# Two transformer blocks on one core: row norms taken by halves of the columns, and the first column tile of the index queries loaded in two contraction halves

## The chip, the core and the metric

The kernel runs on one core of one Trainium2 chip. The metric is the device time of one execution in microseconds (us), taken as the median of several runs. Less is better.

## The reference

Two layers on 256 rows `x` of 1,024 columns, all in float32. Cut to what matters here:

```python
h = rmsnorm(x, g_pre)
... = split_cols(h @ w_in)            # 11,352 columns: index queries iq (512), and 14 more
merged = s_gla * (y_gla @ w_gla_out) + s_dsa * (y_dsa @ w_dsa_out) + s_mem * (y_mem @ w_x_out)
x = x + rmsnorm(merged @ w_o, g_post) # end of the first block
h = rms_norm(x, mix_norm_gain_2)      # start of the second block
...
x = x + merged_2 @ w_out
h2 = rms_norm(x, ffn_norm_gain_2)
x = x + (silu(gate) * up) @ w_down
out = rms_norm(x, final_norm_gain_2)
```

`rmsnorm(x, g)` is `x * rsqrt(mean(x * x over the 1,024 columns) + 1e-6) * g`, row by row. The change touches the norm at the start, the two at the end of the first block (`wo` and `y`), the one ahead of the feed-forward part (`f`), the last one (`o`), and the first projection of the index queries.

## The kernel before, in words

The 256 rows are two row tiles (t = 0, 1) of 128 partitions by 1,024 columns: `xres` holds the residual, `xn` the normalised rows. All weights, about 130 MB, come from memory once. A weight unit (1 MB, 2,048 columns on 128 partitions; some are smaller) is loaded by SyncE (line 1226) into one of five ring slots (`NSLOT`); SyncE issues the load of unit i when TensorE has used unit i - 5. Every unit is then split in two parts for a product that keeps float32 precision: ScalarE writes the high part `w_hi` (`highs`, line 1331, three buffers), VectorE the low part `w_lo` (`lows`, line 1811), and TensorE multiplies three times (`three`, lines 505 to 507: high by high, high by low, low by high). The order of work on each engine is written out by hand: `bank_ready(name)` on ScalarE and VectorE first splits the units up to two past the one that fills the bank `name`, then waits for the bank. `full(name)` is the semaphore of a filled PSUM bank, `read(name)` that of a bank read out.

**A norm** goes through four engines. ScalarE squares a row tile with an accumulator (`squares`, line 1316, plus the read of the accumulator), GpSimd makes `rstd` in two instructions on 128x1 (`rsqrt_mean`: line 1714, multiply and add, then line 1715, power), VectorE multiplies the rows (`scale_rows`, line 1840), and TensorE transposes them, eight 128x128 pieces per row tile (`transpose_tokens`, line 570). ScalarE then writes the high part of the transposed rows with the gain (`high_of_transposed`, line 1354) and VectorE the low part (`low_of_transposed`, line 1848); the products follow.

- **Start.** VectorE copies the transposed parameters first (bank `par0`, line 1862), then scales both row tiles. Unit `small` (0.5 MB, 128 columns) is multiplied first, then `iq0` (1 MB), then small transposes (`ik2`), the transposes of the normalised memory rows (tag `m`), and `iq1`. `project_channels` has the two 128-column tiles c as outer loop and the eight contraction tiles inside.
- **Middle.** `wo0` and `wo1` fill four banks, column half c by row tile t. ScalarE copies them into `xn` (line 1346) and squares a whole row tile when both halves are copied. VectorE multiplies by `rstd` and `g_post` (line 2095) and adds to `xres` (line 2096), which gives `x_mid`. Then the norm `y` on `xres`: `squares`, `rsqrt_mean`, `scale_rows`, transposes, and the products `beta` and `c0` to `c5`, whose results feed a convolution on VectorE. SyncE waits for `x_mid` before it stores the rows and before it loads the units behind `c2` (line 1267).
- **Norm f.** VectorE adds the banks `w2o{c}{t}` into `xres` (line 2402), then the norm.
- **Close.** VectorE adds the banks `wd{c}{t}` into `xres` (line 2431), ScalarE squares each row tile (line 1316), GpSimd makes `rstd`, VectorE writes the result in one instruction for each row tile (line 2435), and SyncE stores it, 512 KB at a time (line 1277).

## Time and profile before

| | |
|---|---|
| median of 3 runs | 929.31 us (929.09 to 931.03) |
| the profiled execution's own time | 927.24 us |
| its span, first to last instruction | 925.4 us |
| TensorE busy | 883.6 us, 95% of the span |
| VectorE busy | 549.7 us, 59% |
| ScalarE busy | 426.5 us, 46% |
| GpSimd busy | 49.7 us, 5% |
| chain that ended last, by engine | TensorE 87%, VectorE 8%, ScalarE 2%, issue 1%, GpSimd 1% |
| granted TensorE clock, mean | 0.988 of full |

TensorE works for all but 41.8 us of the span. The profile also says, for each engine, what it waited for, and shows the instructions in order of time; PE is TensorE's matmuls, DVE is VectorE, ACT is ScalarE, POOL is GpSimd, SPq the queue of SyncE. A line number is one of the kernel before.

### The profile page before, as it was taken

Reading aid. Unit: us, or ns where it says so; the run is one execution under the profiler, and the core shown is the slowest. Engines: PE = TensorE matmul, PEld = TensorE weight load, DVE = VectorE, ACT = ScalarE, POOL = GpSimd, SP = SyncE. Lnnn points to the kernel's source line nnn. Section 1 sums busy time; section 2 is a strip of 40 time slices with the busy share of each in tenths; the row PEclk is TensorE's granted clock in tenths of the full one; section 3 lists DMA queues with packets and bytes.
Section 4 is the critical chain, followed back from the end, with each engine's and each line's share of the span. In section 5 each row is a group of like instructions: output and inputs, shape, how many; then the busy total and the mean of one; then the engine's idle time right before and its main releaser. Section 6 shows DMA issues by size and latency. Waiting matters only on the chain.

```text
span 925.4 us, 13903 instructions
## 1 busy us (share of the span) xinstructions
PE 883.6 (95%) x5834; PEld 773.4 (84%) x5834; DVE 549.7 (59%) x798; ACT 426.5 (46%) x577; POOL 49.7 (5%) x72
## 2 busy tenths in 40 slices
PE   5999999999999999999789999899989899999996
PEld 5998999899998888888679998677877688888885
DVE  4755564573647665654469878754366556666442
ACT  6644444744345444444446515754434444444341
POOL 1000000000020110000010151000000000000000
PEclk9999999999999999999989999999999999999998
DMA  9557743455454544555557665004554465555441
GB/s 302 171 195 221 230 143 137 137 182 182 138 160 160 181 164 155 182 204 198 166 185 161 160 137 184 1 3 139 148 213 149 158 192 190 188 188 185 159 159 46
DMA packets 127492, 151.67 MB, mean 164 GB/s; under 512 B 16919, under 2 KB 93078, under 8 KB 127430
## 3 DMA queue, kind: packets, MB, share of 16 engines
q1 hardware_dynamic: 127290, 150.70, 51.1%
q8 instruction: 46, 0.75, 0.3%
q14 instruction: 16, 0.13, 0.1%
q0 software_dynamic: 64, 0.07, 0.0%
q10 hardware_dynamic: 76, 0.02, 0.0%
HBM read 148.67 MB, written 3.68 MB: 165 GB/s over the span
## 4 chain that ended last, share of the span: by engine, by line
PE 87%; DVE 8%; ACT 2%; issue 1%; POOL 1%; DMA 0%; ACTq 0%; POOLq 0%; DVEq 0%
PE bank L505 25%; PE bank L507 24%; PE bank L506 24%; DVE w_lo L1811 2%; DVE arena L2151 1%; PE bank L570 1%; PE bank L750 1%; ACT w_hi L1331 1%; PE bank L651 1%; PE bank L631 1%; PE bank L975 1%; PE bank L880 1%; PE bank L994 1%; PE bank L1170 1%; ACT h_hi L1354 1%
## 5 line engine op out<-in xcount | busy, mean ns | idle before, releaser
L1811 DVE TENSOR_TENSOR w_lo<-ring,w_hi 128x2048 fp32r<-128x2048 f32 (+2 forms) x133 | 300.7, 2265 | 194.7 <-ACT w_hi L1331 194.5
L1331 ACT ACTIVATE w_hi<-ring 128x2048 fp32r<-128x2048 f32 (+2 forms) x133 | 250.0, 1881 | 138.4 <-PE bank L507 125.8
L505 PE MATMUL bank<-h_hi,w_hi 128*128 128x256 f32 (+1 forms) x640 | 184.9, 289 | 4.0 <-DVE w_lo L1811 2.4
L506 PE MATMUL bank<-h_lo,w_hi 128*128 128x256 f32 (+1 forms) x640 | 181.7, 284 | 0.0
L507 PE MATMUL bank<-h_hi,w_lo 128*128 128x256 f32 (+1 forms) x640 | 181.6, 284 | 0.0
L505 PE MATMUL bank<-w_hi,h_hi 128*128 128x512 f32 (+1 forms) x400 | 155.7, 389 | 0.7 <-DVE h_lo L1848 0.7
L507 PE MATMUL bank<-w_hi,h_lo 128*128 128x512 f32 (+1 forms) x400 | 152.6, 381 | 0.0
L506 PE MATMUL bank<-w_lo,h_hi 128*128 128x512 f32 (+1 forms) x400 | 152.4, 381 | 0.0
L505 PEld LDWEIGHTS bank<-h_hi,w_hi 128*128 128x128 f32 (+1 forms) x640 | 122.8, 192 | 6.8 <-issue 3.3
L506 PEld LDWEIGHTS bank<-h_lo,w_hi 128*128 128x128 f32 (+1 forms) x640 | 123.0, 192 | 0.6 <-issue 0.5
L507 PEld LDWEIGHTS bank<-h_hi,w_lo 128*128 128x128 f32 (+1 forms) x640 | 123.0, 192 | 0.0
L1346 ACT ACTIVATE arena<-bank 128x512 f32<-128x512 f32 (+5 forms) x95 | 48.5, 526 | 110.1 <-PE bank L507 95.4
L505 PEld LDWEIGHTS bank<-w_hi,h_hi 128*128 128x128 f32 x400 | 75.2, 188 | 15.7 <-issue 1.8
L507 PEld LDWEIGHTS bank<-w_hi,h_lo 128*128 128x128 f32 x400 | 75.2, 188 | 14.7
L506 PEld LDWEIGHTS bank<-w_lo,h_hi 128*128 128x128 f32 x400 | 75.3, 188 | 13.7
L1378 ACT ACTIVATE arena<-bank 128x512 f32<-128x512 f32 (+1 forms) x48 | 23.8, 499 | 96.7 <-PE bank L507 96.7
L1714 POOL TENSOR_SCALAR arena<-arena 128x1 f32<-128x1 f32 (+2 forms) x17 | 5.6, 330 | 666.1 <-ACT arena L1316 373.2
L505 PE MATMUL bank<-w_hi,y_hi 128*128 128x512 f32 x96 | 38.6, 402 | 1.2 <-DVE w_lo L1811 1.2
L507 PE MATMUL bank<-w_hi,y_lo 128*128 128x512 f32 x96 | 37.5, 391 | 0.0
L506 PE MATMUL bank<-w_lo,y_hi 128*128 128x512 f32 x96 | 37.5, 390 | 0.0
L1499 ACT ACTIVATE arena<-arena 128x128 f32<-128x128 f32 (+1 forms) x48 | 21.3, 444 | 32.7 <-DVE arena L2027 32.7
L505 PE MATMUL bank<-w_hi,f_hi 128*128 128x512 f32 x88 | 34.3, 390 | 0.0
(311 smaller groups left out, 1198.9 us busy)
## 6 DMA issues: line engine op xcount, KB each, us to landing
ring<-in_w_in SPq DMA_DIRECT2D x60, 1024.0 KB, 4.9
ring<-in_w_gate_up SPq DMA_DIRECT2D x44, 512.0 KB, 4.6
ring<-in_w_down SPq DMA_DIRECT2D x10, 1024.0 KB, 4.9
ring<-in_w_mem_kv SPq DMA_DIRECT2D x8, 1024.0 KB, 6.2
ring<-in_w_gla_out SPq DMA_DIRECT2D x4, 1024.0 KB, 4.9
ring<-in_w_x_out SPq DMA_DIRECT2D x4, 1024.0 KB, 4.9
ring<-in_w_dsa_out SPq DMA_DIRECT2D x4, 1024.0 KB, 5.4
ring<-in_w_o SPq DMA_DIRECT2D x4, 1024.0 KB, 4.9
```

The source lines that it names most:

```text
L505: mm(o, ah, bh, start=start, stop=False, skip_group_check=True)
L506: mm(o, ah, bl, start=False, stop=False, skip_group_check=True)
L507: return mm(o, al, bh, start=False, stop=stop, skip_group_check=True)
L570: ins = nc.tensor.transpose(bank_of(f"T{tag}{j}")[:, 256 * kk + 128 * t:256 * kk + 128 * t + 128], src[:, t, 128 * k:128 * k + 128], ident)
L631: ins = mm(bank[:, 256 * t:256 * t + 256], xq[:, 2 * h + c, 128 * t:128 * t + 128], mk[:, 2 * h + c, :], start=c == 0, stop=c == 1)
L651: ins = mm(bank[:, 256 * c:256 * c + 256], mv[:, m, at:at + 128], probT[:, h % 3, 256 * m:256 * m + 256], start=m == 0, stop=m == 1)
L750: ins = nc.tensor.transpose(bank[:, a:a + 128], rows[:, a:a + 128], ident)
L1331: act(w_hi[:, k % NHI, 0:m], ring[:, order.index(name) % NSLOT, 0:m], ACT.Copy)\
L1346: act(dst, src, ACT.Copy, scale=1.0 if scale is None else scale).then_inc(inc or bank_reader(name), 1)
L1378: act(tnh[:, i % 2, 0:n], src, ACT.Tanh, scale=0.5).then_inc(inc or signal("tanh_done"), 1)
L1499: ins = act(v, v, ACT.Exp, bias=neg_max[:, c:c + 1], scale=-1.0, accum_out=p_sum[:, c:c + 1])
L1811: tt_(w_lo[:, i, 0:m], ring[:, i, 0:m], w_hi[:, k % NHI, 0:m].bitcast(F), ALU.subtract)\
```

## The change

Three edits, one in each of the matters below, and the order of the work around them.

- **Norms by halves.** For `wo`, `y` of the second row tile, `f` and `o`, ScalarE squares 512 columns at a time (`half_squares`). For `wo` it reads the PSUM banks themselves, and the copies into `xn` are gone. GpSimd takes the first half's sum with the 1e-6 (`rsqrt_first`) and adds the second half's to it ahead of the power (`rsqrt_second`): one more 128x1 instruction for each norm and row tile.
- **Gain ahead of the factor.** In the middle VectorE multiplies the bank by `g_post` (`wo_gain`), and then does `xn * rstd + xres` in one instruction for each half (`x_in_the_middle`). At the close it multiplies by the last gain as each bank comes, and the last step is `result`, a multiplication by `rstd` for each half; SyncE stores 256 KB at a time, four times. In `f` and `o` the first halves' sums of both row tiles stand ahead of the second halves'.
- **Start.** VectorE scales row tile 0 ahead of the copy of `par0`. The unit `iq0` becomes `iq0a` and `iq0b`, contraction tiles 0 to 3 and 4 to 7, 0.5 MB each and each in its own ring slot, and `project_channels_by_parts` has the contraction tile as outer loop and the column tile inside. The matmuls are the same in number and shape. All later units sit one ring slot further on.

```diff
-        units_of("iq", w1, W1_OFF["iq"], 2)
+        for half in range(2):
+            unit(f"iq0{'ab'[half]}", piece(w1, W1_OFF["iq"], 256, 0, 4 * half, 4 * half + 4))
+        units_of("iq", w1, W1_OFF["iq"] + 256, 1, 1)
...
+            def project_channels_by_parts(name, x):
+
+                bank = open_bank(name)
+                for part, k0 in (("a", 0), ("b", 4)):
+                    wh, wl = split_unit(name + part, 256)
+                    for k in range(k0, k0 + 4):
+                        for c in range(2):
+                            s = slice(128 * c, 128 * c + 128)
+                            ins = three(bank[:, 256 * c:256 * c + 256], (wh[:, k - k0, s], wl[:, k - k0, s]),
+                                        (x[0][:, k, :], x[1][:, k, :]), k == 0 and c == 0, k == KT - 1)
+                    if part == "a":
+                        part_done(name + part, ins)
+                done(name, ins)
+                unit_used[name + "b"] = full(name)
...
-            project_channels("iq0", h_parts)
+            project_channels_by_parts("iq0", h_parts)
...
-                    sp.wait_ge(signal("x_mid"), 2)
+                    sp.wait_ge(signal("x_mid"), 4)
...
-                sp.wait_ge(signal("result"), t + 1)
-                sp.dma_start(out[0, 128 * t:128 * t + 128, :], xn[:, t, :]).then_inc(signal("out_done"), 16)
-            sp.wait_ge(signal("out_done"), 32)
+                for c in range(2):
+                    sp.wait_ge(signal("result"), 2 * t + c + 1)
+                    sp.dma_start(out[0, 128 * t:128 * t + 128, 512 * c:512 * c + 512], xn[:, t, 512 * c:512 * c + 512])\
+                        .then_inc(signal("out_done"), 16)
+            sp.wait_ge(signal("out_done"), 64)
...
+            def half_squares(tag, src, col, c, t):
+
+                n = square_count[tag] = square_count.get(tag, 0) + 1
+                i = col + 2 * c + t
+                act(probT[:, c, :], src, ACT.Square, accum_out=sumsq[:, i:i + 1]).then_inc(signal(f"sumsq_{tag}"), 1)
+                sc.wait_ge(signal(f"sumsq_{tag}"), n)
...
+            sc.wait_ge(*read("par0"))
             high_of_transposed("x", h_hi)
-            highs(2)
+            highs(3)
...
-            copy_wide("wo0", xn, 0)
-            for t in range(TT):
-                copy(f"wo1{t}", xn[:, t, 512:1024])
-                squares("wo", xn, 4, t, read(f"wo1{t}"))
-            highs(splits_by["wo11"] + 2)
-            for t in range(TT):
-                squares("y", xres, 0, t, (signal("x_mid"), t + 1))
+            for c in range(2):
+                for t in range(TT):
+                    bank_ready(f"wo{c}{t}")
+                    half_squares("wo", bank_of(f"wo{c}{t}")[:, :], 4, c, t)
+            squares("y", xres, 2, 0, (signal("x_mid"), 2))
+            square_count["y"] = 1
+            for c in range(2):
+                sc.wait_ge(signal("x_mid"), c + 3)
+                half_squares("y", xres[:, 1, 512 * c:512 * c + 512], 0, c, 1)
...
-            highs(splits_by["w2o11"] + 2)
-            for t in range(TT):
-                squares("f", xres, 4, t, read(f"w2o1{t}"))
+            for c in range(2):
+                for t in range(TT):
+                    highs(splits_by[f"w2o{c}{t}"] + 2)
+                    sc.wait_ge(*read(f"w2o{c}{t}"))
+                    half_squares("f", xres[:, t, 512 * c:512 * c + 512], 4, c, t)
...
-                squares("o", xres, 6, t, read(f"wd1{t}"))
+            for c in range(2):
+                for t in range(TT):
+                    sc.wait_ge(*read(f"wd{c}{t}"))
+                    half_squares("o", xres[:, t, 512 * c:512 * c + 512], 0, c, t)
...
+            def rsqrt_first(tag, col, t, n):
+
+                gp.wait_ge(signal(f"sumsq_{tag}"), n)
+                step(nc.gpsimd.tensor_scalar(var[:, col + t:col + t + 1], sumsq[:, col + t:col + t + 1], 1 / D, EPS,
+                                             ALU.mult, ALU.add))
+
+            def rsqrt_second(tag, col, t, n):
+
+                i = slice(col + 2 + t, col + 3 + t)
+                gp.wait_ge(signal(f"sumsq_{tag}"), n)
+                step(nc.gpsimd.tensor_scalar(var[:, i], sumsq[:, i], 1 / D, var[:, col + t:col + t + 1], ALU.mult, ALU.add))
+                nc.gpsimd.tensor_tensor(rstd[:, i], var[:, i], mhalf, ALU.pow).then_inc(signal(f"rstd_{tag}"), 1)
...
-            for t in range(TT):
-                rsqrt_mean("wo", 4 + t, 1, D, t + 1)
-            for t in range(TT):
-                rsqrt_mean("y", t, 1, D, t + 1)
+            rsqrt_first("wo", 4, 0, 1)
+            rsqrt_first("wo", 4, 1, 2)
+            rsqrt_second("wo", 4, 0, 3)
+            rsqrt_second("wo", 4, 1, 4)
+            rsqrt_mean("y", 2, 1, D, 1)
+            rsqrt_first("y", 0, 1, 2)
+            rsqrt_second("y", 0, 1, 3)
...
+            for name, col in (("f", 4), ("o", 0)):
+                for t in range(TT):
+                    rsqrt_first(name, col, t, t + 1)
+                for t in range(TT):
+                    rsqrt_second(name, col, t, TT + t + 1)
...
+            scale_tile("x", xn, xres, 0, 0)
             ve.wait_ge(*full("par0"))
             nc.vector.tensor_copy(par[:, 0:38], bank_of("par0")[:, 0:38]).then_inc(reader("par0"), 1)
+            scale_tile("x", xn, xres, 0, 1)
             ve.wait_ge(*read("par0"))
             tsc(g_gla_half, g_gla, 0.5, None, ALU.mult)
-            scale_rows("x", xn, xres, 0)
             lows(1)
             low_of_transposed("x", h_lo, h_hi)
-            lows(2)
+            lows(3)
...
+            def wo_gain(c, t):
+                s = slice(512 * c, 512 * c + 512)
+                ve.wait_ge(signal("sumsq_wo"), 2 * c + t + 1)
+                tt_(xn[:, t, s], bank_of(f"wo{c}{t}")[:, :], g_post[:, s], ALU.mult).then_inc(reader(f"wo{c}{t}"), 1)
+
+            def x_in_the_middle(t):
+                r = rstd_of("wo", 6, t)
+                for c in range(2):
+                    s = slice(512 * c, 512 * c + 512)
+                    ve.wait_ge(*read(f"wo{c}{t}"))
+                    stt(xres[:, t, s], xn[:, t, s], r, xres[:, t, s], ALU.mult, ALU.add).then_inc(signal("x_mid"), 1)
+
+            ve.wait_ge(signal("g_post_in"), 16)
+            for t in range(TT):
+                bank_ready(f"wo0{t}")
+                wo_gain(0, t)
+            lows(splits_by["wo11"] + 1)
+            ve.wait_ge(signal("x_again"), 16)
+            wo_gain(1, 0)
+            x_in_the_middle(0)
+            wo_gain(1, 1)
+            x_in_the_middle(1)
+            ve.wait_ge(signal("x_mid"), 4)
+            scale_tile("y", xn, xres, 2, 0)
+            scale_tile("y", xn, xres, 2, 1)
             lows(splits_by["wo11"] + 2)
-            ve.wait_ge(signal("g_post_in"), 16)
-            ve.wait_ge(signal("x_again"), 16)
-            for t in range(TT):
-                r = rstd_of("wo", 4, t)
-                step(stt(xn[:, t, :], xn[:, t, :], r, g_post, ALU.mult, ALU.mult))
-                tt_(xres[:, t, :], xres[:, t, :], xn[:, t, :], ALU.add).then_inc(signal("x_mid"), 1)
-
-
-            scale_rows("y", xn, xres, 0)
...
-            lows(splits_by["Tf3"] + 2)
-            scale_rows("f", xn, xres, 4)
+            scale_rows("f", xn, xres, 6)
...
+            ve.wait_ge(signal("g_fin_in"), 16)
+
+            def result(t):
+                r = rstd_of("o", 2, t)
+                for c in range(2):
+                    o = xn[:, t, 512 * c:512 * c + 512]
+                    tsc(o, o, r, None, ALU.mult).then_inc(signal("result"), 1)
+
             for c in range(2):
+                s = slice(512 * c, 512 * c + 512)
                 for t in range(TT):
                     bank_ready(f"wd{c}{t}")
-                    v = xres[:, t, 512 * c:512 * c + 512]
+                    v = xres[:, t, s]
                     tt_(v, v, bank_of(f"wd{c}{t}")[:, :], ALU.add).then_inc(reader(f"wd{c}{t}"), 1)
-            ve.wait_ge(signal("g_fin_in"), 16)
+                    ve.wait_ge(*read(f"wd{c}{t}"))
+                    step(tt_(xn[:, t, s], v, g_fin[:, s], ALU.mult))
             for t in range(TT):
-                r = rstd_of("o", 6, t)
-                stt(xn[:, t, :], xres[:, t, :], r, g_fin, ALU.mult, ALU.mult).then_inc(signal("result"), 1)
+                result(t)
```

VectorE's instructions at the start, from the parameters' copy to the memory rows (x4 and the like count equal rows; `w_lo<-ring,w_hi` is a unit's low part, `h_lo` the low part of the transposed rows). Before:

```order
L1862 COPY arena<-bank 128x38
L1864 TENSOR_SCALAR arena<-arena 128x2
L1840 TENSOR_SCALAR arena<-arena 128x1024 x2
L1811 TENSOR_TENSOR w_lo<-ring,w_hi 128x1024
L1848 SCALAR_TENSOR_TENSOR h_lo<-bank,arena,h_hi 128x256 x8
L1811 TENSOR_TENSOR w_lo<-ring,w_hi 128x2048
L1840 TENSOR_SCALAR arena<-arena 128x1024 x2
```

The same place in the changed kernel:

```order
L1891 TENSOR_SCALAR arena<-arena 128x1024
L1918 COPY arena<-bank 128x38
L1891 TENSOR_SCALAR arena<-arena 128x1024
L1921 TENSOR_SCALAR arena<-arena 128x2
L1863 TENSOR_TENSOR w_lo<-ring,w_hi 128x1024
L1903 SCALAR_TENSOR_TENSOR h_lo<-bank,arena,h_hi 128x256 x8
L1863 TENSOR_TENSOR w_lo<-ring,w_hi 128x1024 x2
L1891 TENSOR_SCALAR arena<-arena 128x1024 x2
```

The first row tile is scaled ahead of the copy, and the low part of `iq0` is two pieces of half the size.

VectorE's instructions in the middle, from the split of `beta` (128x448) on. Before:

```order
L1811 TENSOR_TENSOR w_lo<-ring,w_hi 128x448
L1811 TENSOR_TENSOR w_lo<-ring,w_hi 128x2048
L2095 SCALAR_TENSOR_TENSOR arena<-arena 128x1024
L2096 TENSOR_TENSOR arena<-arena 128x1024
L2095 SCALAR_TENSOR_TENSOR arena<-arena 128x1024
L2096 TENSOR_TENSOR arena<-arena 128x1024
L1840 TENSOR_SCALAR arena<-arena 128x1024 x2
L1848 SCALAR_TENSOR_TENSOR h_lo<-bank,arena,h_hi 128x256 x8
```

The same place in the changed kernel:

```order
L2149 TENSOR_TENSOR arena<-bank,arena 128x512 x2
L1863 TENSOR_TENSOR w_lo<-ring,w_hi 128x448
L2149 TENSOR_TENSOR arena<-bank,arena 128x512
L2156 SCALAR_TENSOR_TENSOR arena<-arena 128x512 x2
L2149 TENSOR_TENSOR arena<-bank,arena 128x512
L2156 SCALAR_TENSOR_TENSOR arena<-arena 128x512 x2
L1891 TENSOR_SCALAR arena<-arena 128x1024 x2
L1863 TENSOR_TENSOR w_lo<-ring,w_hi 128x2048
L1903 SCALAR_TENSOR_TENSOR h_lo<-bank,arena,h_hi 128x256 x8
```

Two of the four multiplications by the gain stand ahead of the split of `beta`, and the split of `c0` (128x2048) has moved from ahead of the norm to between the scaled rows and the low part of their transposes.

## Rows read from the trace of the kernel before

**Rows 1.** Waits of TensorE, whole span: us in total, times, longest us

```profile
PE bank L570 <- DVE arena L1840: 11.1, 3, 7.3
```

**Rows 2.** Timeline, start: start us, us, engine line op out<-in xcount [idle before <-releaser]

```profile
6.06 0.55 POOL L1715 TENSOR_TENSOR arena<-arena 128x1 f32<-128x1 f32 x1
7.50 1.57 DVE L1840 TENSOR_SCALAR arena<-arena 128x1024 f32<-128x1024 f32 x2
8.30 3.68 PE L570 MATMUL bank<-arena 128*128 128x128 f32 x16 [1.15 <-DVE arena L1840]
9.82 1.22 DVE L1811 TENSOR_TENSOR w_lo<-ring,w_hi 128x1024 fp32r<-128x1024 f32 x1 [0.75 <-ACT w_hi L1331]
10.74 3.03 ACT L1354 ACTIVATE h_hi<-bank,arena 128x256 fp32r<-128x256 f32 x8 [0.95 <-PE bank L570]
11.61 3.22 DVE L1848 SCALAR_TENSOR_TENSOR h_lo<-bank,arena,h_hi 128x256 fp32r<-128x256 f32 x8 [0.57 <-ACT h_hi L1354]
15.60 2.29 DVE L1811 TENSOR_TENSOR w_lo<-ring,w_hi 128x2048 fp32r<-128x2048 f32 x1 [0.76 <-ACT w_hi L1331]
17.94 0.38 PE L505 MATMUL bank<-h_hi,w_hi 128*128 128x256 f32 x1 [2.08 <-DVE w_lo L1811]
17.48 1.06 ACT L1316 ACTIVATE arena<-arena 128x1024 f32<-128x1024 f32 x1 [1.92 <-DMA arena<-in_mem]
21.05 0.75 DVE L1840 TENSOR_SCALAR arena<-arena 128x1024 f32<-128x1024 f32 x1 [0.71 <-POOL arena L1715]
19.85 1.91 ACT L1331 ACTIVATE w_hi<-ring 128x2048 fp32r<-128x2048 f32 x1
```

**Rows 3.** Timeline of TensorE: transposes of the memory rows; first index products

```profile
26.16 1.97 PE L570 MATMUL bank<-arena 128*128 128x128 f32 x16
34.62 3.44 PE L611 MATMUL bank<-arena 64*128 64x128 f32 x32
```

**Rows 4.** Busy time by stretch: length, PE, PEld, DVE, ACT, POOL, clock, DMA share, GB/s

```profile
20.00:21.00 1.00, 1.00 (x6) 1.00 (x6) 0.33 (x1) 1.00 (x1) 0.92 (x2) 0.50 1.10 353
45.00:60.00 15.00, 15.00 (x127) 15.00 (x126) 10.29 (x13) 6.24 (x5) 0.00 (x0) 1.00 0.62 211
464.00:466.00 2.00, 0.00 (x0) 0.00 (x0) 1.56 (x2) 1.01 (x2) 1.30 (x1) 0.50 0.12 47
470.00:471.00 1.00, 0.41 (x4) 0.44 (x5) 1.00 (x4) 1.00 (x4) 0.00 (x0) 1.00 1.08 379
```

**Rows 5.** Timeline, middle

```profile
456.23 0.60 ACT L1346 ACTIVATE arena<-bank 128x512 f32<-128x512 f32 x1 [0.74 <-PE bank L507]
460.60 0.19 ACT L1316 ACTIVATION_READ_ACCUMULATOR arena<-arena 128x1 f32 x1
460.40 1.23 DVE L2096 TENSOR_TENSOR arena<-arena 128x1024 f32<-128x1024 f32 x1
460.87 0.80 POOL L1714 TENSOR_SCALAR arena<-arena 128x1 f32<-128x1 f32 x1 [1.94 <-ACT arena L1316]
463.77 1.53 POOL L1715 TENSOR_TENSOR arena<-arena 128x1 f32<-128x1 f32 x1
466.23 3.46 PE L570 MATMUL bank<-arena 128*128 128x128 f32 x16 [7.32 <-DVE arena L1840]
469.57 3.23 DVE L1848 SCALAR_TENSOR_TENSOR h_lo<-bank,arena,h_hi 128x256 fp32r<-128x256 f32 x8 [1.74 <-ACT h_hi L1354]
```

**Rows 6.** Timeline, norm f

```profile
728.33 3.35 PE L570 MATMUL bank<-arena 128*128 128x128 f32 x16 [2.60 <-DVE arena L1840]
```

**Rows 7.** Timeline, close; last row: stores' time from issue to landing

```profile
917.56 0.69 DVE L2431 TENSOR_TENSOR arena<-arena,bank 128x512 f32<-128x512 f32 x1 [0.67 <-PE bank L507]
919.57 0.85 POOL L1714 TENSOR_SCALAR arena<-arena 128x1 f32<-128x1 f32 x1 [0.60 <-ACT arena L1316]
921.09 1.28 DVE L2435 SCALAR_TENSOR_TENSOR arena<-arena 128x1024 f32<-128x1024 f32 x1 [0.72 <-POOL arena L1715]
...
DMA to landing us min/median/max: 2.6/2.8/3.0
```

12 lines of the change are left out of this document (5 added, 7 removed).

## The prediction

> **What bounds the kernel now.** I read the shares first: TensorE is busy for 883.6 of 925.4 us, so only its 41.8 us of idle time, and its time at a low clock, can be had. Then TensorE's waits: the largest by far, 11.1 us in three places, is for scaled rows, ahead of the transposes of a norm [rows 1]. The timeline shows them: 1.15 us at the start [rows 2], 7.32 in the middle [rows 5], 2.60 at norm f [rows 6]; at the start 2.08 us more go to the split of `iq0` [rows 2]. From the memory rows' transposes on, TensorE has no idle stretch for hundreds of us; one such stretch is shown [rows 4]. So an earlier start of a product-bound stretch moves everything behind it, while nothing but TensorE's own products stands in it. The close is a chain of VectorE, ScalarE, GpSimd and a store, with nothing beside it [rows 7].
>
> **The start.** The factor of row tile 0 is there at 6.06 + 0.55 = 6.61, yet VectorE scales only at 7.50, behind the copy of `par0` [rows 2]. Moved ahead, it scales until 7.4, the transposes start at 7.45 and not at 8.30, and the first bank comes 0.85 us earlier. VectorE gains less of it: its split of `small` ends at 9.82 + 1.22 = 11.04, so `h_lo` starts at 11.05 and not at 11.61, and ends at 14.3. ScalarE's `h_hi` ends 0.85 us earlier, at 12.9.
>
> The split of `iq0` now: `w_hi` cost one 128x2048 (1.91 by a row of its kind) and `w_lo` 2.29, one behind the other, and the products began at 17.94 [rows 2]. In halves ScalarE is done with `iq0a` at 14.0 (half of 1.91 and some fixed time, about 1.06), beside `h_lo`; VectorE's half costs 1.22, the duration of the 128x1024 split, and ends at 15.5. `iq0b` ends at 16.75, inside the 2.9 us that the first half's 24 products take at 0.123 (1.97 / 16, [rows 3]). So `iq0` starts at 15.55, 2.4 us earlier. Two halves cost 2.44 us on VectorE for 2.29, beside other work.
>
> From there to the memory rows' transposes went 26.16 - 17.94 = 8.2 us, but part of it at a granted clock of 0.50 [rows 3, 4]; of 3.3 us at that level half, 1.6 us, is loss. Before it TensorE had stood idle for the 2.08 us, which now go. I take the loss as gone: the transposes can start at 22.15 (23.8 if the clock drops again). Their rows are ready at 21.05 + 0.75 = 21.8 in both kernels, since the memory rows land at 17.48 [rows 2]; no bound, just. With 1.97 us they end at 24.1. Now `iq1` is late next: ScalarE splits it from 19.85 on; it now copies `small` first (about 0.36) and ends at 22.1, VectorE at 24.4. So `iq1` starts at 24.4 in place of 26.16 + 1.97 = 28.1. ScalarE then has the high parts of the memory rows and a weight unit ahead of the copy of `iq1`, some 0.4 us too late, so the index products start at 31.3, not 34.62 [rows 3]: **3.3 us**. Bounds: 1.5 (the low clock comes back, and one DMA lands 1 us late) and 4.0. The extra ring slot costs a unit of lead only while DMA is full: the loads for `mk1` now wait for `small` to be used, at 15.3, and `mk1` is wanted at 28.7. I cost it and the extra DMA issue at nothing; if that cover is gone, they cost the 1 us above.
>
> **The middle.** The bank `wo10` is full at 456.2. ScalarE no longer copies (0.60) and then squares 1,024 columns (1.06); it squares 512 from the bank, for which I take the copy's 0.60, and 0.19 for the accumulator [rows 5]. The last product of `wo1` ends at 466.23 - 7.32 = 458.91. The sum of `wo11` is ready at 459.7, its factor 0.8 later (0.55 for the power, an estimated 0.25 ahead of it), at 460.5, while VectorE multiplies that bank by the gain (0.69, as the 128x512 with a bank at the close [rows 7]). Two fused halves at an estimated 0.72 (half of 1.28, and fixed time [rows 7]) end at 462.0: `x_mid` is whole. The squares of `y0` ran from 459.7 to 460.9; its factor is held by the fused halves and comes at 462.2 to 462.6; scaled by 463.0 to 463.35. Transposes start at 463.1, not at 466.23: 3.1 us. For `y1`, the last half's squares end at 462.8, its factor comes at 463.8, its rows at 464.6; row tile 0's eight transposes, at 3.46 / 16 each, last until 464.8, so this hides. The step that is moved bites: the split of `c0`, 2.29 us, now stands between scaled rows and `h_lo`, until 466.95. Without it `h_lo` would start 3.34 us behind the first transpose, as at 469.57, so at 466.45. It loses 0.5: **2.6 us** stay. SyncE's wait is for all four halves of `x_mid` and ends 2.9 us earlier; the loads queued behind it gain likewise. The convolution behind `c0` is a chain of VectorE that starts from the bank of `c0`, and moves as a whole. Bounds: 0.8 (the clock, below) and 3.3.
>
> GpSimd shows the price of company: a 128x1 instruction at 460.87 took 0.80 us and ended at 461.67, with VectorE's 128x1024 from two SBUF tensors at 461.63; the power at 463.77 took 1.53, for 0.55 alone [rows 2, 5]. The Trainium skill (GPSIMD Engine Reference, Key points) says that GpSimd shares its SBUF interfaces with VectorE and contends with instructions that have two SBUF inputs or run in a 2-port mode; the trace agrees. It speaks against this change, whose fused halves and final multiplications are of these kinds; without such holding the total below would be some 0.8 us better, and I keep the holding in.
>
> **Norm f.** Only ScalarE's last two squares shrink, by 1.06 - 0.60 = 0.46 us, and they chain: **0.5 us** (0 to 0.9) of the 2.60 [rows 6].
>
> **The close.** The first halves are done long before. Behind the last product, VectorE has one more 128x512 multiplication (0.69) for each bank, hidden: the one of `wd10` ends at 917.6, as the last addition starts (917.56 before), and that of `wd11` beside ScalarE. Addition until 918.3, squares and accumulator of 512 until 919.1, GpSimd held by `result(0)` until 919.6, power until 920.1 to 920.5, then two multiplications of 512 at about 0.45 (half of the 128x1024 scale's 0.75, and fixed time): the last ends at 921.1 to 921.4. Before it was 921.09 + 1.28 = 922.37 [rows 2, 7]. The last store has 256 KB and not 512; at 379 GB/s [rows 4] that is 0.7 less of the 2.8 to landing, of which I count 0.5. **1.5 us** (0.7 to 2.3).
>
> **The sum:** 3.3 + 2.6 + 0.5 + 1.5 = 7.9, taken as 7.8. The profiled execution itself took 927.24 and would take 919.4. It lay 2.1 us under the median of 929.31; the same gain from that gives **921.5 us**.
>
> **The rivals.**
> - *The low clock spoils part of it.* In the middle the clock was 0.50 at 464 to 466 and 1.00 at 470 to 471 [rows 4], after little but transposes. Restarted earlier, with TensorE idle again until `h_lo` at 467, it may stay low through `beta` and half of `c0`: transposes take 0.216 us at the low level and 0.123 at the high one [rows 3, 5], so 40 products at 0.1 more cost 4 us less some cover, 2.5; or the start's 1.6 us stays. Then 924.5. The Trainium skill (TensorE: Matmul & The Clock Gate, Part 4: PE-mode transpose) says that transposes do not bring the high level; the rise here came while hardly anything else had run, so the trace speaks against it. By that rule this case would be the rule.
> - *The start does nothing.* `iq0a` and the copy ahead save time, but the memory rows land at 17.48 whatever TensorE does [rows 2], and if the loads behind them (`mk0`, `mk1`) land later, ScalarE, which takes things in a fixed order, holds the copies. The gain is then 4.6: 924.7.
> - *Slower.* One mechanism: TensorE keeps the lower level after the restart of `iq0` or `beta`. Each 1 MB unit has 48 products, 0.095 us dearer each: 4.6 us a unit. It decides from 1.7 units on, where 7.8 is used up; over three units the time is 935. For it: the clock did drop in the start. Against: each time it came back within some 3 us of work.
> - *No change that can be told:* the gains are eaten at a place where VectorE is the pace, in the convolution: 928.5.
>
> **The numbers.** My forecast, gains of 5.5 to 10, has 0.73; the low clock 0.10, the start 0.09, slower 0.04, none 0.04. A measurement can tell about 0.2%, 1.9 us. Both middle rivals are still faster: faster 0.92, same 0.04, slower 0.04. The range reaches from 919.0 (nearly the best bounds) to 925.5, which takes in the two rivals at 924.5 and 924.7.
>
> **What would show it.** Right: TensorE's first `iq0` product near 15.6 with no wait over 0.5 us ahead of it, no 0.50 clock at 19 to 22; the index products near 31.3; in the middle 4.2 us of wait ahead of the transposes, not 7.32, and `h_lo` starting right behind a 128x2048 split; 2.1 ahead of those of norm f; from the last product to the span's end 6.4 us, not 7.9. Wrong: index products after 33, or a middle wait over 5.5 us, or a clock of 0.50 in products of `iq0`, `beta` or `c0`.

## The result, and the profile after

| | before | changed |
|---|---|---|
| median, with the first comparison | 928.98 us (925.52 to 931.03, 7 runs) | 923.16 us (922.37 to 924.77, 7 runs) |
| ratio, 95% interval | | 0.9944 (0.9927 to 0.9962) |
| profiled execution's own time, span | 927.24, 925.4 us | 922.42, 920.6 us |
| median, on another chip | 929.39 us (927.09 to 931.3, 11 runs) | 923.52 us (922.92 to 924.52, 5 runs) |
| ratio there | | 0.9938 (0.9923 to 0.9953) |

The change makes the kernel 5.8 us faster by the medians, and 5.2 (3.5 to 6.8) by the ratio. I forecast 7.8 and 921.5 us; 923.16 lies inside the range that I gave, 919.0 to 925.5. Between the two profiled executions, whose rows follow, the gain is 4.8.

TensorE's waits of the changed kernel, as [rows 1]: engine, line, what it waited for: us in total, times, longest.

```profile
PE bank L587 <- DVE arena L1891: 7.8, 4, 4.7
PE bank L507 <- DVE w_lo L1863: 2.6, 4, 1.2
PE bank L507 <- DVE h_lo L1903: 2.5, 3, 0.9
```

The wait for scaled rows fell from 11.1 to 7.8 us, and the longest from 7.3 to 4.7.

Timeline of the start of the changed kernel, as [rows 2, 3]: start us, us, engine, line, operation, out<-in, count, idle before.

```profile
6.73 0.75 DVE L1891 TENSOR_SCALAR arena<-arena 128x1024 f32<-128x1024 f32 x1 [6.73 <-POOL arena L1750]
7.54 3.53 PE L587 MATMUL bank<-arena 128*128 128x128 f32 x16 [0.42 <-DVE arena L1891]
...
14.05 2.35 DVE L1863 TENSOR_TENSOR w_lo<-ring,w_hi 128x1024 fp32r<-128x1024 f32 x2
...
15.33 0.39 PE L507 MATMUL bank<-h_hi,w_hi 128*128 128x256 f32 x1 [0.16 <-DVE w_lo L1863]
...
17.96 1.06 ACT L1335 ACTIVATE arena<-arena 128x1024 f32<-128x1024 f32 x1 [3.00 <-DMA arena<-in_mem]
...
22.06 1.97 PE L587 MATMUL bank<-arena 128*128 128x128 f32 x16
...
24.89 0.39 PE L507 MATMUL bank<-h_hi,w_hi 128*128 128x256 f32 x1 [0.86 <-DVE w_lo L1863]
31.66 3.44 PE L628 MATMUL bank<-arena 64*128 64x128 f32 x32
```

`iq0` begins at 15.33 after 0.16 us of wait (2.08 before), the memory rows' transposes at 22.06 (26.16), `iq1` at 24.89, and the index products at 31.66 (34.62): 2.96 us earlier.

The middle, as [rows 5].

```profile
457.81 1.41 DVE L2156 SCALAR_TENSOR_TENSOR arena<-arena 128x512 f32<-128x512 f32 x2 [0.33 <-POOL arena L1764]
458.03 0.58 POOL L1749 TENSOR_SCALAR arena<-arena 128x1 f32<-128x1 f32 x1 [0.26 <-ACT arena L1335]
458.69 0.94 POOL L1750 TENSOR_TENSOR arena<-arena 128x1 f32<-128x1 f32 x1
459.74 0.75 DVE L1891 TENSOR_SCALAR arena<-arena 128x1024 f32<-128x1024 f32 x1 [0.51 <-POOL arena L1750]
460.64 3.65 PE L587 MATMUL bank<-arena 128*128 128x128 f32 x16 [4.66 <-DVE arena L1891]
461.96 2.28 DVE L1863 TENSOR_TENSOR w_lo<-ring,w_hi 128x2048 fp32r<-128x2048 f32 x1
464.16 3.22 DVE L1903 SCALAR_TENSOR_TENSOR h_lo<-bank,arena,h_hi 128x256 fp32r<-128x256 f32 x8
465.18 0.29 PE L507 MATMUL bank<-h_hi,w_hi 128*56 128x256 f32 x1 [0.89 <-DVE h_lo L1903]
```

The wait is 4.66 us, 2.66 less. The split of `c0` at 461.96 stands ahead of `h_lo`, which starts 3.52 us behind the first transpose and not 3.34 as before: 0.18 is given back. GpSimd's two small instructions took 0.58 and 0.94 us beside the fused halves of VectorE (0.19 and 0.55 alone).

Norm f, as [rows 6].

```profile
722.13 0.69 POOL L1763 TENSOR_SCALAR arena<-arena 128x1 f32<-128x1 f32 x1 [0.30 <-ACT arena L1345]
722.83 1.06 PE L587 MATMUL bank<-arena 128*128 128x128 f32 x8 [2.35 <-DVE arena L1891]
724.30 1.97 PE L587 MATMUL bank<-arena 128*128 128x128 f32 x8 [0.41 <-DVE arena L1891]
...
726.98 0.77 PE L507 MATMUL bank<-w_hi,h_hi 128*128 128x512 f32 x1 [0.71 <-DVE h_lo L1903]
```

The wait is 2.35 us, 0.25 less. But the second eight transposes take 1.97 us for the 1.06 of the first eight, and the products behind go at the same low clock.

The close, as [rows 7].

```profile
914.16 0.69 DVE L2511 TENSOR_TENSOR arena<-arena,bank 128x512 f32<-128x512 f32 x1
...
915.77 0.46 POOL L1763 TENSOR_SCALAR arena<-arena 128x1 f32<-128x1 f32 x1 [0.48 <-ACT arena L1345]
916.31 0.60 POOL L1764 TENSOR_TENSOR arena<-arena 128x1 f32<-128x1 f32 x1
916.94 0.88 DVE L2504 TENSOR_SCALAR arena<-arena 128x512 f32<-128x512 f32 x2 [0.43 <-POOL arena L1764]
```

VectorE ends at 917.82, 3.86 us after TensorE's last product (913.96); before these were 922.37 and 4.85 (917.52). From the last product to the span's end it is now 6.64 us, not 7.88: 1.24 less.

Now the clock. Busy time by stretch in both kernels: length, PE, PEld, DVE, ACT, POOL, granted clock, DMA share, GB/s. The four stretches are the start, the middle, a place ahead of the split of `z` in the second block, and norm f. First before, then changed.

```profile
17.00:24.00 7.00, 6.06 (x38) 6.06 (x39) 4.60 (x4) 5.77 (x7) 1.76 (x4) 0.76 1.07 335
455.00:475.00 20.00, 11.78 (x70) 10.13 (x69) 13.15 (x16) 12.53 (x23) 6.70 (x11) 0.83 0.49 159
680.00:695.00 15.00, 12.39 (x53) 10.00 (x52) 9.22 (x9) 4.31 (x4) 0.00 (x0) 0.89 0.45 158
718.00:740.00 22.00, 18.69 (x85) 15.09 (x83) 11.79 (x15) 10.83 (x15) 1.75 (x4) 0.92 0.45 150
```

```profile
17.00:24.00 7.00, 7.00 (x57) 6.26 (x55) 2.96 (x3) 5.55 (x7) 1.78 (x4) 1.00 1.07 331
455.00:475.00 20.00, 14.44 (x101) 13.05 (x100) 15.18 (x19) 11.27 (x22) 5.06 (x11) 0.83 0.51 162
680.00:695.00 15.00, 12.38 (x49) 9.95 (x48) 10.38 (x10) 4.99 (x4) 0.00 (x0) 0.89 0.41 141
718.00:740.00 22.00, 18.53 (x76) 14.79 (x76) 12.73 (x17) 8.59 (x15) 2.07 (x4) 0.84 0.45 145
```

Length times (1 - clock) is what a stretch lost in granted clock: before 1.7, 3.4, 1.7 and 1.8 us; changed 0, 3.4, 1.7 and 3.5. What the change took away at the start has come back at norm f. There it falls on products: from the first `gu0` product to the transposes of `fT0` it was 16.45 us before, and is 18.30. The four gains add up to 2.96 + (2.66 - 0.18) + 0.25 + 1.24 = 6.9; less 1.85, and 0.2 in small differences, that is the 4.8 of the two profiles.

So my question for the runs: does the low clock at norm f belong to the change, or to the execution? Theory P: the fall follows idle time, and where it begins and ends differs between executions of one program. Theory Q: the edit at norm f, or the earlier arrival there, brings it.

### The profile page after: what moved, and what is told of

It reads as the page before. It is cut to its first block, busy times and chain, and to the rows that moved or that the text cites. A ratio compares the mean times of both kernels' runs of the same rounds, so it can differ in the third digit from the quotient of the medians.

```text
span 920.6 us, 13959 instructions
## 1 busy us (share of the span) xinstructions
PE 884.1 (96%) x5834; PEld 773.3 (84%) x5834; DVE 551.9 (60%) x809; ACT 426.5 (46%) x588; POOL 50.5 (5%) x79
## 4 chain that ended last, share of the span: by engine, by line
PE 87%; DVE 8%; ACT 2%; DMA 1%; issue 1%; SPq 1%; POOL 0%; POOLq 0%; DVEq 0%; ACTq 0%
PE bank L507 25%; PE bank L509 25%; PE bank L508 24%; DVE w_lo L1863 2%; DVE arena L2223 1%; DMA arena<-in_mem 1%; PE bank L767 1%; PE bank L668 1%; PE bank L648 1%; PE bank L992 1%; PE bank L897 1%; PE bank L1011 1%; ACT w_hi L1359 1%; SPq L1243 1%; PE bank L1187 1%
## 5 line engine op out<-in xcount | busy, mean ns | idle before, releaser
L1863 DVE TENSOR_TENSOR w_lo<-ring,w_hi 128x2048 fp32r<-128x2048 f32 (+1 forms) x134 | 300.9, 2250 | 186.4 <-ACT w_hi L1359 186.0
L1359 ACT ACTIVATE w_hi<-ring 128x2048 fp32r<-128x2048 f32 (+1 forms) x134 | 250.2, 1870 | 136.2 <-PE bank L509 122.4
L1374 ACT ACTIVATE arena<-bank 128x512 f32<-128x512 f32 (+5 forms) x91 | 46.2, 523 | 100.8 <-PE bank L509 86.0
L509 PE MATMUL bank<-w_hi,f_lo 128*128 128x512 f32 x88 | 34.2, 389 | 0.0
```

The costliest lines, as they stand in the source:

```text
L509: return mm(o, al, bh, start=False, stop=stop, skip_group_check=True)
L1359: act(w_hi[:, k % NHI, 0:m], ring[:, order.index(name) % NSLOT, 0:m], ACT.Copy)\
L1374: act(dst, src, ACT.Copy, scale=1.0 if scale is None else scale).then_inc(inc or bank_reader(name), 1)
L1863: tt_(w_lo[:, i, 0:m], ring[:, i, 0:m], w_hi[:, k % NHI, 0:m].bitcast(F), ALU.subtract)\
```

## The experiments

Times are medians of up to 12 runs; each ratio is to the kernel before on the same chip, of which there are 11 to 35 runs. "Low clock lost" is worked out as above. Where a text says fT, it means the time from the first transpose of norm f to the first of `fT0`.

**The four edits, each alone on the kernel before.** The start (`iq0` in halves, scaling ahead of the copy of `par0`):

```diff
-            project_channels("iq0", h_parts)
+            project_channels_by_parts("iq0", h_parts)
...
+            scale_tile("x", xn, xres, 0, 0)
```

> The start alone: row tile 0 scaled ahead of par0, iq0 in two contraction halves; everything else as before. Theory (the parts add up, each moves all behind it): 3.0 us faster, as the index products stand 2.96 us earlier in the changed kernel's trace, so ratio 0.9968; no stretch at clock 0.50 around 19 to 22 us, and the middle wait still 7.3 us. Rival (the start's gain is lost later, in the VectorE-paced convolution or at the clock): under 1 us, ratio over 0.999.

The middle (halves, gain first, split of `c0` behind):

```diff
+                    half_squares("wo", bank_of(f"wo{c}{t}")[:, :], 4, c, t)
...
+            x_in_the_middle(1)
```

> The middle alone: half squares for wo and y, gain ahead of the factor, the split of c0 behind the scaled rows; the rest as before. Theory: the wait ahead of the transposes falls from 7.3 to 4.7 us and the first beta product comes 2.5 us earlier; 2.5 us faster, ratio 0.9973. Rival (the clock at norm f takes part of it back): 0.6 to 1 us faster only, with a low clock in the first products of gu0.

Norm f:

```diff
-            for t in range(TT):
-                squares("f", xres, 4, t, read(f"w2o1{t}"))
+                    half_squares("f", xres[:, t, 512 * c:512 * c + 512], 4, c, t)
```

> Norm f by halves alone. Theory P (the low clock in the first gu0 products of the changed kernel is a matter of when the chip lowers the clock, not of this edit): wait 0.25 us shorter and the time within 0.2% of before, in either direction. Theory Q (the half-wise sums themselves bring it, since row tile 0's transposes now run alone and an idle gap of 0.4 us follows): 1.5 to 2 us slower, ratio 1.0018, with products of gu0 at half clock for about 4 us.

The close:

```diff
+                    step(tt_(xn[:, t, s], v, g_fin[:, s], ALU.mult))
...
+                result(t)
```

> The close alone: squares by halves, gain ahead of the factor, four stores of 256 KB. Theory: 1.25 us faster (last VectorE instruction 1.06 us earlier against the last product, the smaller store 0.2), ratio 0.9987. Rival (the extra multiplications and held GpSimd steps eat it): no change.

| alone | median | ratio | what its own profile shows |
|---|---|---|---|
| start | 927.06 | 0.9974 (0.9961 to 0.9988) | index products at 32.32 |
| middle | 926.94 | 0.9978 (0.9963 to 0.9992) | wait 4.66, first product behind it 4.54 us after the first transpose (4.36 before) |
| norm f | 928.61 | 1.0001 (0.9985 to 1.0016) | wait 2.34 |
| close | 928.48 | 0.9994 (0.9979 to 1.0009) | last VectorE instruction 3.85 us after the last product, span's end 7.22 |

Start and middle are gains of 2.4 and 2.0 us; norm f gives none that can be told; the close 0.6, inside its interval. Together 0.53%, and the whole change has 0.56 and 0.62: no loss from having them together can be told, though each of these ratios is known to some 0.15% only.

None of the first, second and fourth touches norm f, and all three lost 3.4 to 3.5 us of clock there and have an fT of 22.17, 22.46 and 22.44 us (20.52 in the profile of before, 22.45 in that of the changed kernel). So norm f's low clock is not the edit's, and it needs no earlier arrival either: the run of norm f's edit alone comes to those transposes at 728.05 (728.33 before) and has an fT of 22.27, and a kernel without any of the four edits (the one filled ahead of `iq0`, below) comes at 728.79 and has 22.09. The odd one is the profile of before.

The profile of the middle alone brought a second thing. Its start is that of the kernel before, yet its index products start at 33.12 and not at 34.62:

```profile
12.60 0.55 PE L505 MATMUL bank<-h_hi,w_hi 128*128 128x256 f32 x1 [0.65 <-DVE h_lo L1878]
16.57 0.41 PE L505 MATMUL bank<-h_hi,w_hi 128*128 128x256 f32 x1
33.12 3.44 PE L611 MATMUL bank<-arena 64*128 64x128 f32 x32
```

```profile
17.00:24.00 7.00, 7.00 (x54) 6.72 (x54) 4.46 (x4) 5.67 (x7) 1.76 (x4) 1.00 1.06 334
```

The products of `small` take 0.41 us each up to about 17.5, where the profile of before has 0.28 from the second on. Because they end late, TensorE doesn't stand idle ahead of `iq0`, and no fall follows: what is slow first is saved after. I call a start early where `small` is fast from its second product on, and late where it is slow up to some 16 to 17.6 us. So the kernel before has two kinds of start, with index products at 34.4 to 34.6 (early, three profiles) or at 33.12 (late, one), and so has the changed one: 31.1 to 31.7 (early, five profiles), or 32.32 (late, the start alone). The start's gain is some 3.0 us where both rise early, and 0.8 where both rise late.

**The changed kernel once more, without its norm f, and with fillers.** The first is the unchanged file on a second chip. The second takes the edit of norm f back:

```diff
-                    half_squares("f", xres[:, t, 512 * c:512 * c + 512], 4, c, t)
+                squares("f", xres, 4, t, read(f"w2o1{t}"))
```

> The changed kernel itself, a second profile. If the low clock at norm f comes from where the idle time falls against the chip's own beat (theory P), this profile may show it elsewhere or not at all, and then a span up to 1.9 us shorter or equal; if it belongs to the edit (theory Q), the first gu0 products stand at half clock for 4 us again.

> The changed kernel with norm f as before (whole-row squares, two-instruction factor), all else changed. Theory P: within 0.5 us of the changed kernel (its wait is 0.25 us longer). Theory Q: 1.5 to 2 us faster than the changed kernel, with full clock in the first gu0 products.

The changed kernel again 923.52 us; without norm f's edit 923.53 (ratio 0.9936, 0.9919 to 0.9954), wait 2.60, fT 22.22, low clock lost at norm f as much. The edit is worth nothing that a run can tell, and theory Q falls in its first form.

The changed kernel's second profile shows the rival of my prediction in the middle:

```profile
455.00:475.00 20.00, 14.45 (x91) 13.53 (x89) 14.45 (x18) 10.49 (x20) 4.99 (x10) 0.74 0.51 161
```

5.2 us of clock lost and not 3.4: products of 0.41 us go on until 468.3, over most of `beta`. A clock of 0.50 in products of `beta` stood among my signs of being wrong, and here it came. From the first of them to the transposes of `gtok` (the first group after those of `c0`) it took 10.37 us for 8.84. Of the six profiles with the edit of the middle and without fillers there, three have 8.84 or 8.85, three 10.35 to 10.80; of five without the edit, four have 8.84 to 8.86, one 10.59. The numbers are too few to say that the edit makes it more frequent.

The third puts nine 128x512 products into the idle time ahead of norm f's transposes; their result is overwritten.

```diff
+                for _ in range({'f': 9}.get(tag, 0)):
+                    mm(bank_of(f"T{tag}3")[:, :], h_hi[:, 0, 0:128], h_hi[:, 0:2, :].rearrange("p a b -> p (a b)"),
+                       start=True, stop=True, skip_group_check=True)
```

> The changed kernel with nine extra 128x512 products in TensorE's wait ahead of norm f's transposes, whose results are overwritten by the transposes. They take 9 x 0.227 = 2.0 of the 2.35 us of wait. If the idle time causes the low clock at norm f: no stretch under 1.00 between 715 and 735, transposes at 0.12 us each, first gu0 products at 0.23, and 1.9 us faster than the changed kernel where that had lost them, about 0.8 on the transposes alone. If the transposes cause it: the clock falls all the same, no gain.

922.69 us (0.9924, 0.9908 to 0.994). The stretch of transposes in its profile, and the one behind it; then the fillers and the first `gu0` product:

```profile
724.00:728.00 4.00, 2.19 (x17) 1.75 (x17) 1.85 (x4) 1.97 (x6) 0.57 (x2) 1.00 0.57 196
728.00:732.00 4.00, 4.00 (x11) 3.12 (x12) 3.24 (x7) 2.86 (x4) 0.00 (x0) 0.57 0.00 0
```

```profile
721.52 2.20 PE L583 MATMUL bank<-h_hi 128*128 128x512 f32 x9
...
727.93 0.58 PE L507 MATMUL bank<-w_hi,h_hi 128*128 128x512 f32 x1 [1.34 <-DVE h_lo L1906]
```

Half of the low clock is gone (1.7 us lost, not 3.5), but what is left falls wholly on products, and fT is 22.05, no better. As it was stated, theory P failed here: there should have been no stretch under 1.00. Behind the fillers came transposes and 0.21 + 0.47 + 1.34 us of waits, and then the fall. The six runs lie at 922.55 to 923.61 but for one, at 919.83 with a mean granted clock of 0.997: no more than 3.2 us of granted clock lost in all, though the middle's wait was not filled. So much do single executions differ.

**`iq1` split ahead of the memory rows.**

```diff
-            highs(3)
+            highs(4)
...
-            lows(3)
+            lows(4)
```

> The changed kernel with the split of iq1 ahead of the memory rows' squares on ScalarE (which stood idle for 3.0 us there, waiting for the memory rows) and ahead of their scaling on VectorE. Theory: iq1's wait of 0.86 us goes, and ScalarE comes earlier to m_hi and the copy of iq1; 0.9 us faster than the changed kernel. Rival (the memory rows' squares are pushed back): no gain, since the split ends at 16.9 and the rows land at 17.96, expected not to happen.

924.25 us (0.9938, 0.9922 to 0.9953), as the changed kernel. Its profile rose late, as that of the start alone, and from the memory rows' transposes to the index products both take 8.47 us: rising late, `iq1` isn't waited for in either, and there is nothing to gain. In the changed kernel's profile, which rose early, this stretch is 9.60 us. No profile with `iq1` early rose early, so what it is worth there stays open.

**Fillers in all of these stretches.** On the kernel before, ahead of `iq0` alone:

```diff
+                for _ in range(9 if name == "iq0" else 0):
+                    mm(bank[:, :], h_hi[:, 0, 0:128], h_hi[:, 0:2, :].rearrange("p a b -> p (a b)"),
+                       start=True, stop=True, skip_group_check=True)
```

> The kernel before, with nine 128x512 products (0.227 us each, 2.04 us; their results are overwritten) in the 2.08 us in which TensorE stood idle ahead of iq0. Theory P (the clock falls in the start because TensorE stood idle there, as it did not in the profile of the middle alone, where small ran at the low level until 17 us and left no idle time): no 0.50 clock at 18 to 23; the index products start at 33.1 and not at 34.4 to 34.6; the rest as before. If small ends late in this execution, the nine products push iq0 back instead, and the index products start at 34 or later. Theory Q (the fall is a matter of the transfers or of the place in the program): the low clock at 18 to 23 is there all the same, index products at 34.5. Time: 0 to 1.5 us less than before by P, and no change by Q.

On the changed kernel, ahead of the transposes of both norms and behind them (`{'f': 9, 'y': 19}` in the edit above, and):

```diff
+            for _ in range(4):
+                mm(bank[:, :], mg_hi[:, 0, 0:128], mg_hi[:, 0:2, :].rearrange("p a b -> p (a b)"),
+                   start=True, stop=True, skip_group_check=True)
...
+                for _ in range(5 if j == 0 else 0):
+                    mm(bank_of("gu00")[:, :], m2_hi[:, 0, 0:128], m2_hi[:, 0:2, :].rearrange("p a b -> p (a b)"),
+                       start=True, stop=True, skip_group_check=True)
```

> The changed kernel with overwritten 128x512 products in its idle stretches: 19 ahead of the middle's transposes (4.3 of 4.66 us) and 4 behind them (0.89 us of wait), 9 ahead of norm f's transposes (2.0 of 2.35 us) and 5 behind them (1.34 us of wait with the earlier filler). Theory P (the clock falls for idle time and comes back for products; what filled norm f alone left was the stretch of transposes and waits behind): no 0.50 clock at 457 to 470 nor at 722 to 733; beta and c0 all at the high level, from the first h product to the copy stretch 8.84 us and never 10.4; from the transposes of norm f to those of fT 20.5 us in place of 22.1; the whole 2 to 3.5 us under the changed kernel, near 920.5. Theory Q (transposes do not count as work, and hold the clock down whatever stands around them): one low stretch is left in each place, 1 us less than the changed kernel or no difference, 922.5 to 923.5.

The same with `iq1` early, and the kernel before with fillers in all places:

> As the kernel with all fillers, and iq1 split ahead of the memory rows (which removes the 0.5 to 0.9 us that TensorE waits for it). If the two add up: the index products start at 30.8 to 31.2 and not at 31.1 to 31.7, the whole another 0.3 to 0.6 us under the kernel with all fillers, near 920.0 by theory P and 922 to 923 by theory Q. If moving the split only moves the wait to the copies behind it, as the profile of it alone cannot tell since small ran slowly there, it is the same as the kernel with all fillers.

> The kernel before with overwritten 128x512 products in all its idle stretches of that kind: 9 ahead of iq0, 30 ahead of the middle's transposes (6.8 of 7.32 us) and 3 behind them, 10 ahead of norm f's transposes (2.3 of 2.60 us) and 5 behind them. Against the changed kernel with all fillers it has the change's own gains, with the clock at the high level in both. By what the profiles show these are 1.9 at the start (index products 33.2 against 31.3), 2.5 in the middle, 0.3 at norm f and 1.2 at the close, together 5.9: it should run in 925.9 us, no 0.50 clock anywhere, first middle transpose 4.6 us behind that of the changed kernel. If the forecast's own terms were right and the clock alone spoiled them (7.8), it runs in 927.8. If it runs in 924 or less, part of the change's gain was the removal of low-clock stretches and not of waits.

| | median | ratio | low clock lost |
|---|---|---|---|
| before, filled ahead of `iq0` | 929.04 | 1.0006 (0.9995 to 1.0017) | start 0, middle 6.8, `z` 1.7, norm f 3.5 |
| before, filled everywhere | 925.48 | 0.995 (0.9935 to 0.9965) | 0 |
| changed, filled everywhere | 919.99 | 0.9907 (0.9887 to 0.9927) | 0 |
| changed, filled, `iq1` early | 919.14 | 0.9905 (0.9885 to 0.9924) | 0 |

The start of the first of them:

```profile
15.74 2.23 PE L515 MATMUL bank<-h_hi 128*128 128x512 f32 x9
...
33.17 3.44 PE L614 MATMUL bank<-arena 64*128 64x128 f32 x32
```

`small` rose early here. With the idle time filled, the fall behind 18 us is gone and the index products come at 33.17, where 33.1 was expected by P. Of the profiles that rise early, the three with that wait of 2 us have the fall, and this one and the five with the start's edit, all without the wait, don't: there the fall followed idle time. The time as a whole is not less, and that is not for this one profile alone: the 11 runs have a mean granted clock of 0.987, as have the 17 of before beside them, and the ratio leaves at most 0.5 us. One reason is in sight. Where `small` rises late there is no wait to fill, and the nine products push `iq0` back; how many executions that was isn't known.

The changed kernel with all fillers, same four stretches:

```profile
17.00:24.00 7.00, 7.00 (x58) 6.46 (x57) 3.29 (x3) 5.67 (x7) 1.77 (x4) 1.00 1.06 335
455.00:475.00 20.00, 18.22 (x125) 15.80 (x124) 15.26 (x20) 11.26 (x22) 5.01 (x10) 1.00 0.52 163
680.00:695.00 15.00, 12.06 (x56) 9.87 (x56) 11.35 (x12) 6.01 (x6) 0.00 (x0) 1.00 0.42 142
718.00:740.00 22.00, 21.14 (x100) 16.95 (x100) 13.46 (x18) 10.73 (x17) 2.07 (x4) 1.00 0.45 143
```

```profile
455.41 4.47 PE L583 MATMUL bank<-h_hi 128*128 128x512 f32 x19
460.15 1.09 PE L590 MATMUL bank<-arena 128*128 128x128 f32 x8 [0.27 <-DVE arena L1900]
...
462.55 1.17 PE L837 MATMUL bank<-mg_hi 128*128 128x512 f32 x4
464.78 0.30 PE L507 MATMUL bank<-h_hi,w_hi 128*56 128x256 f32 x1 [1.06 <-DVE h_lo L1912]
```

The clock is 1.00 in all four. Products of `beta` and `c0` take 8.85 us, fT 20.43. Expected were 8.84 and 20.5, and 920.5 as a whole. This kernel computes the same, and is the version that beats both: 8.7 us faster than before, and faster than the changed one by 3.5 us in medians, 2.9 by the ratios to before (0.9907 and 0.9938). Early `iq1` on top can't be told from it; its profile rose late, with index products at 32.06 and not at the 30.8 to 31.2 expected.

The fillers don't always hold the clock. Of the 16 runs filled everywhere 15 have a mean granted clock of 0.996 to 0.998; the end of the program, where TensorE has nothing left to do, takes 0.002 to 0.003 of that in the two profiles from which I reckon it (1.8 us of granted clock changed, 2.6 before). One, with early `iq1`, has 0.993 and took 923.86 us, where the other five took 918.6 to 919.4. And the profile of the changed kernel filled is the fastest of its four runs, at 918.24; the other three took 919.95 to 920.22 with 0.996 and 0.997, so a short fall may have been in them.

The two filled kernels were to set the change's gain apart from the clock. By their medians it is 925.48 - 919.99 = 5.5 us; by their ratios, each to before on its own chip, 0.43%, or 4.0. Expected were 5.9. The two intervals leave about 1.7 to 6.3 us, so my 7.8 isn't met, but whether the change is worth as much with the clock out of both as with it can't be told. Nor is the start of the filled kernel before clean. In its profile `small` rose late, the fillers stood behind it, and the index products came at 34.84, where 33.2 was expected and a late start without fillers has 33.12:

```profile
17.69 2.21 PE L515 MATMUL bank<-h_hi 128*128 128x512 f32 x9
...
34.84 3.44 PE L617 MATMUL bank<-arena 64*128 64x128 f32 x32
```

That the filled kernel before is still 4.2 us faster than before shows that the low clock was a cost there all along.

At `z`, where nothing was edited and no filler stands, TensorE waits 2.6 us in all kernels. The clock fell there in nine of the 14 profiles, but not in those of the middle alone, the close alone and the three kernels filled everywhere. The fall has a price: from the first product behind that wait to the next transposes it is 12.4 to 12.7 us in the nine, and 11.0 or 11.1 in the five. The changed kernel, then the same filled everywhere:

```profile
695.39 1.04 PE L793 MATMUL bank<-arena 128*128 128x128 f32 x8
```

```profile
682.32 0.50 PE L507 MATMUL bank<-w_hi,z_hi 128*128 128x512 f32 x1 [2.61 <-DVE z_lo L2465]
693.34 1.04 PE L796 MATMUL bank<-arena 128*128 128x128 f32 x8
```

The first products are at 682.74 and 682.32, so this is 12.65 and 11.02. Of the 4.2 us between these two profiles' spans, 2.0 are won at norm f, 1.6 here and 0.35 ahead of the index products. So a good third comes from a place without fillers. That fillers further ahead keep the clock up here isn't shown, as two profiles without any have no fall either. Idle time alone doesn't decide it. What does was not tested.

## Why the prediction was right, and where not

The mechanisms were right: an earlier start of a product-bound stretch moves all behind it. The sum was too large by 2.0 us. Point by point:

- **Start, 3.3 us.** `iq0` at 15.33 (15.55 forecast), transposes at 22.06 (22.15), `iq1` at 24.89 (24.4), index products at 31.66 (31.3). For the profile at hand the term holds: 2.96. What failed is the sentence "I take the loss as gone", not in the changed kernel (no fall there in any profile) but in the kernel before: it has that loss only in executions where the clock rises early. In the others the start gives 0.8 us. Alone it gave 2.4.
- **The extra load, nothing.** That holds as far as can be seen. ScalarE had the memory rows at 17.96 and not at 17.48, but they come at 17.5 to 17.9 in the six profiles without the extra load and at 17.4 to 18.0 in the six with it in which ScalarE waits for them, so this is no price of the load. What I had wrong is that it doesn't matter. ScalarE splits `iq1` behind them, so in the five early starts of the changed kernel `iq1` follows them by 6.93 or 6.94 us, from 17.39 and 24.32 to 17.96 and 24.89, and the index products follow `iq1` by 6.8. That is the 0.49 us by which `iq1` is later than my 24.4, and it covers the 0.36 of the index products: I had taken the landing of one profile for a fixed time.
- **Middle, 2.6 us.** 2.66 - 0.18 = 2.48. The two halves of it were each off and met by luck: the wait is 4.66 and not 4.2, since I took the early end of the range for the factor and GpSimd was held at both instructions (0.58 + 0.94, for 0.19 + 0.55, is 0.78 more); the moved split cost 0.18 and not 0.5, as it starts 1.32 us behind the first transpose, where the forecast has 1.56 (466.95 - 2.29 - 463.1), and `h_lo` follows it without a gap.
- **Norm f, 0.5 us.** The wait shrank by 0.25. The step that failed counted only ScalarE's squares: GpSimd's chain for the first row tile, from the sum to the factor, has grown from 0.92 to 1.09 us, from 726.41 to 727.33 before and 720.74 to 721.83 now. And alone it is worth nothing that can be measured.
- **Close, 1.5 us.** 1.24: VectorE ends 3.86 us after the last product, forecast 3.6 to 3.9 (4.85 before). From there to the span's end it is 2.78 us for 3.03, so the smaller stores took 0.25 off and not 0.5. In the profile of the close alone this was 3.37, longer than before, and the gain there only 0.66.
- **The rival "the low clock spoils part of it"** had 0.10. In the pair of profiles it took 1.85 us at norm f, a place that I hadn't named, and it is the profile of before that was lucky there: of eleven profiles without fillers behind norm f's transposes, this one had 16.45 us from the first `gu0` product to the transposes of `fT0`, and the other ten 18.0 to 18.4. In the middle it came true in three of the six profiles, for 1.5 to 2.0 us, with the clock at 0.50 in products of `beta`, one of my signs of being wrong. This was a part of the forecast, not a rival to it.
- **The rival "the start does nothing"** is refuted by 31.66. "Slower" too: the low level never outlasted one unit of products. "No change that can be told": the gain at the first product behind the middle's transposes is 5.41 us (470.59 to 465.18), and at the first transposes behind `z` still 5.25 (700.64 to 695.39).

The runs gave 5.8 us where I had 7.8. Of the missing 2.0, the waits of middle, norm f and close were 0.12 + 0.25 + 0.26 = 0.6 smaller than forecast. The start, alone, gave 2.4 for 3.3, by its two kinds of beginning. The rest, 0.5, is within what two medians of such runs differ by; how often the middle's low clock on products came in the runs isn't known. The runs do have their granted clock on record, and it is a little higher with the change: 0.9890 and 0.9884 on average, where before has 0.9865 (35 runs) and 0.9855 (11 runs). That is 2.3 to 2.7 us of granted clock. How much of it is time, and how much fell on waits and on the idle end, which is shorter now, isn't shown. So a part of the 5.8 may be low clock removed.

The Trainium skill (TensorE: Matmul & The Clock Gate, Part 1: The HAM clock gate) says that what the chip watches runs freely and doesn't start with the kernel, so that the same kernel sees the change at another point in each run. The traces agree: `small` ran fast from its second product on in one profile, and from 17.6 in another, with the same code there. On transposes (the Trainium skill, same page, Part 4: PE-mode transpose, weighed in the prediction) the evidence stands divided: in the changed kernel's profile the clock fell at 457.9 and came back at 464.8, with nothing between but the 16 transposes; in its second profile the same 16 transposes were followed by products of `beta` at the low level until 468.3; and in the run with fillers ahead of norm f alone it fell after transposes and waits that followed full work.

## What to carry to other kernels

Where TensorE waits some 2 to 7 us, count the clock with the wait. In this kernel a fall often came with or behind such a wait, and where it reached the first products it cost up to 2 us more. Shortening the wait from 7.3 to 4.7 us in the middle and from 2.6 to 2.35 at norm f didn't remove it. With overwritten products in the waits and behind the transposes the three profiles have no fall ahead of the end, and the kernels were 2.9 to 3.5 us (changed) and 4.2 us (before) faster; in the profiles of the changed kernel a good third of the gain is from `z`, where none was put in, and one of the 16 runs was slow all the same. And one profile of before is one throw: the start and norm f happened to run one way in it, and so did the landing of the memory rows, so look at a second one, or bound the terms that rest on a clock seen once.

## What was not expected of the hardware

- The time that a fixed program spends at the low clock varies between executions. Of the kernel before's 35 runs on one chip, the nine with a mean granted clock of 0.983 or 0.984 took 930.9 to 931.4 us, and the three with 0.990 took 925.6 or 925.7. Filled everywhere it took 923.78 to 925.85.
- Ahead of 17 us the granted clock is shown as 1.00 while products can take the low level's time. Busy time by stretch, kernel with the middle alone:

```profile
12.00:17.00 5.00, 4.40 (x21) 4.43 (x21) 4.24 (x9) 3.53 (x6) 0.00 (x0) 1.00 1.08 371
```

  The product at 16.57 in it takes 0.41 us, for 0.28 at the high level. At the start one has to read the products and not the clock.
- A slow beginning can be the better one: rising late, the start of the kernel before had its index products 1.3 to 1.5 us earlier than rising early, where no idle time and no fall followed.
